# Where forty-eight groups of modulation rows are computed: the last eight move from the gaps about a layer norm into the pairs of the gated unit

## The reference, cut to what matters

```python
def adaln_params(cond, w, b):
    mod = (jax.nn.silu(cond) @ w + b)[:, None, :]
    return jnp.split(mod, 6, axis=-1)

def conformer_conv(h, w_in, b_in, dw_w, dw_b, ln_g, ln_b, w_out, b_out):
    a, gt = jnp.split(h @ w_in + b_in, 2, axis=-1)
    z = a * jax.nn.sigmoid(gt)
    z = depthwise_conv(z, dw_w, dw_b)          # 31 taps
    z = jax.nn.silu(layer_norm(z, ln_g, ln_b))
    return z @ w_out + b_out
...
    h = h + g1 * rms_norm(y, norm_g[i, 1])
    f = conv_ffn(rms_norm(h, norm_g[i, 2]) * (1.0 + sc2) + sh2, ...)
```

## Time and profile before

| | |
|---|---|
| median of three timed executions | 3034.64 us |
| profiled execution, its own time | 3032.49 us |
| its span in the profile | 3030.7 us |
| PE busy | 2747.4 us (91%) |
| DVE busy | 2064.8 us (68%) |
| ACT busy | 1280.9 us (42%) |
| mean granted TensorE clock | 0.954 of full speed |

### The profile page before, as it was taken

The page is one execution under the profiler, slowest core; times in us unless marked ns, Lnnn a source line. Parts: engine busy times, 40 slices in busy tenths (PEclk is TensorE's granted clock), DMA queues, the critical chain, the costliest instruction groups (busy, mean ns, idle before and its releaser), DMA issues. The chain is left out here.

```text
span 3030.7 us, 44962 instructions
## 1 busy us (share of the span) xinstructions
PE 2747.4 (91%) x17388; PEld 2473.3 (82%) x17388; DVE 2064.8 (68%) x2883; ACT 1280.9 (42%) x1888; POOL 132.4 (4%) x177
## 2 busy tenths in 40 slices
PE   5898888999999989999988498999899999999996
PEld 3888776999998989999976366777889999878785
DVE  3899988888975565655745547666478457584665
ACT  4231244433445353333431527777554334443332
POOL 0000000000000000000000002333000000000000
PEclk7999988999999999999998798999999999999998
DMA  6444422222221212222221120000122322233332
GB/s 261 152 160 146 149 102 89 79 84 92 90 77 65 81 56 89 79 87 94 71 89 56 42 76 9 1 1 1 56 84 85 97 97 88 94 95 120 97 97 83
DMA packets 66519, 263.14 MB, mean 87 GB/s; under 512 B 6960, under 2 KB 7216, under 8 KB 60080
## 3 DMA queue, kind: packets, MB, share of 16 engines
q1 hardware_dynamic: 58368, 213.17, 21.4%
q0 software_dynamic: 5760, 41.95, 3.9%
q10 hardware_dynamic: 2224, 5.69, 0.5%
HBM read 256.58 MB, written 4.19 MB: 86 GB/s over the span
## 5 line engine op out<-in xcount | busy, mean ns | idle before, releaser
L1603 PE MATMUL PS<-a_hi,w_hi 128*128 128x322 f32 (+7 forms) x3584 | 922.8, 326 | 113.5 <-DVE w_lo L962 58.4
L1603 PE MATMUL PS<-a_lo,w_hi 128*128 128x322 f32 (+7 forms) x3584 | 905.4, 321 | 0.0
L1603 PE MATMUL PS<-a_hi,w_lo 128*128 128x322 f32 (+7 forms) x3584 | 904.0, 321 | 0.0
L1603 PEld LDWEIGHTS PS<-a_hi,w_hi 128*128 128x128 f32 x3584 | 617.8, 194 | 168.7 <-DVE w_lo L962 73.2
L1603 PEld LDWEIGHTS PS<-a_lo,w_hi 128*128 128x128 f32 x3584 | 620.5, 194 | 25.2 <-issue 2.1
L1603 PEld LDWEIGHTS PS<-a_hi,w_lo 128*128 128x128 f32 x3584 | 617.1, 193 | 25.3
L962 DVE TENSOR_TENSOR w_lo<-raw,w_hi 128x1024 fp32r<-128x1024 f32 (+2 forms) x380 | 443.3, 1171 | 224.1 <-ACT w_hi L481 217.5
L481 ACT ACTIVATE w_hi<-raw 128x1024 fp32r<-128x1024 f32 (+2 forms) x380 | 385.7, 1015 | 1.6 <-DVE zB L1474 1.4
L1603 PE MATMUL PS<-z_hi,w_hi 128*128 128x320 f32 (+1 forms) x1056 | 301.3, 340 | 30.4 <-DVE z_lo L1351 28.3
L1603 PE MATMUL PS<-z_lo,w_hi 128*128 128x320 f32 (+1 forms) x1056 | 299.2, 338 | 0.0
L1603 PE MATMUL PS<-z_hi,w_lo 128*128 128x320 f32 (+1 forms) x1056 | 299.0, 338 | 0.0
(11 more groups left out here) (242 smaller groups left out, 3126.0 us busy)
## 6 DMA issues: line engine op xcount, KB each, us to landing
raw<-wstream SPq DMA_DIRECT2D x380, 512.0 KB, 3.5
ada_slot<-adastream POOLq DMA_DIRECT2D x40, 1024.0 KB, 5.2
ada_first<-adastream SPq DMA_DIRECT2D x4, 2048.0 KB, 19.8
h<-xT SPq DMA_DIRECT2D x1, 2640.0 KB, 14.6
h<-xT ACTq DMA_DIRECT2D x1, 2480.0 KB, 9.9
out<-h ACTq DMA_DIRECT2D x1, 2048.0 KB, 9.3
out<-h SPq DMA_DIRECT2D x4, 512.0 KB, 2.7
rope_sb<-rope ACTq DMA_DIRECT2D x1, 1024.0 KB, 4.9
```

Of the source, the lines that this page charges most:

```text
L1603: last = MM(PS[:, 2 * j + m, 0:n], wt[:, j, k, :], mv[:, k, m * n:(m + 1) * n], start=(k == 0 and p_ == 0), stop=(k == tiles - 1 and p_ == 2))
```

## The change

The four constants that said where the groups go become two tuples with the number of groups in each pair of the two gated stages. Stage A has 2, 2, 3, 3, 3, 3, 3, 2 (21 groups, 8 to 28), stage B has 3, 3, 3, 3, 2, 2, 2, 1 (19 groups, 29 to 47). A third group stands in the middle of a pair's first unit, ahead of k-tile 4; ACT copies it before it evacuates that unit. Nothing is left between stage B and cm but the turn of the last group, and nothing in the join.

```diff
-ADA_A, ADA_B, ADA_GAP, ADA_JOIN = 8, 24, 40, 42
+ADA_A, ADA_B = (2, 2, 3, 3, 3, 3, 3, 2), (3, 3, 3, 3, 2, 2, 2, 1)
...
                     for i in range(8):
-                        q, g, ga = q0 + i, x["g"] + i, x["ada"] + 2 * i
+                        q, g, rows = q0 + i, x["g"] + i, x["ada_n"][i]
+                        ga = x["ada"] + sum(x["ada_n"][:i])
+                        if rows == 3:
+                            ada_row_out(ga)
+                            ga += 1
...
                         split(q + 1, 1)
-                        ada_row_out(ga + 1)
+                        if rows > 1:
+                            ada_row_out(ga + 1)
...
                 if kind == "cm":
-                    for g in range(ADA_GAP, ADA_JOIN):
-                        ada_row_out(g)
                     cm_units(x)
                 if kind == "join":
-                    ada_row_out(ADA_JOIN)
                     root(s + 1, MIX, 2)
-                    for g in range(ADA_JOIN + 1, ADA_JOIN + 3):
-                        ada_row_out(g)
...
                     for m in range(4):
-                        if ADA_JOIN + 3 + m < N_MOD:
-                            ada_row_out(ADA_JOIN + 3 + m)
                         tiles = join_tiles(x, m)
...
-            def ada_group(g):
-
+            def ada_next(g):
+
+                if g > ADA_FIRST:
+                    ada_turn(g - 1)
                 ada_rows(g, ada_slot[g % 2])
-                ada_turn(g)
...
-                        unit(q, 0, a_hi, a_lo, w, KT, fresh=x["n"] - 1 if i == 0 else None)
+                        unit(q, 0, a_hi, a_lo, w, KT, {4: lambda g=ga: ada_next(g)} if rows == 3 else {},
+                             fresh=x["n"] - 1 if i == 0 else None)
...
-                        if ga > ADA_FIRST:
-                            ada_turn(ga - 1)
-                        ada_rows(ga, ada_slot[ga % 2])
+                        ga += rows == 3
+                        ada_next(ga)
                         unit(q, 1, a_hi, a_lo, w, KT)
-                        ada_turn(ga)
-                        ada_rows(ga + 1, ada_slot[(ga + 1) % 2])
+                        if rows > 1:
+                            ada_next(ga + 1)
                 if kind == "cm":
-                    ada_turn(ADA_GAP - 1)
-                    for g in range(ADA_GAP, ADA_JOIN):
-                        ada_group(g)
+                    ada_turn(N_MOD - 1)
...
                 if kind == "join":
-                    ada_rows(ADA_JOIN, ada_slot[ADA_JOIN % 2])
                     pe.wait_ge(evacuated, 2 * q0)
                     average_summed(7, rms[:, 0:MIX], MIX, 2)
-                    ada_turn(ADA_JOIN)
-                    for g in range(ADA_JOIN + 1, ADA_JOIN + 3):
-                        ada_group(g)
                     for k in range(KT):
                         pe.wait_ge(squared, x["sq"] + 8 + k + 1)
                         last = ones_product(t_mix[:, k], MIX, 2, k == 0, k == KT - 1)
                     last.then_inc(norm_step, 1)
-                    for g in range(ADA_JOIN + 3, N_MOD):
-                        ada_group(g)
```

More of the change, by code:

```diff
@@ L101, in plan @@
     ph = [dict(kind="pre", layer=0, which=0, chunk=glu_a, w=GA, t="T", first=True),
-          dict(kind="glu", chunk=glu_a, pairs=8, units=[("glu", 0, 8)], ada=ADA_A, host=pre_gb), pre_gb,
-          dict(kind="glu", chunk=glu_b, pairs=8, units=[("glu", 0, 8)], ada=ADA_B, host=ln_a), ln_a,
+          dict(kind="glu", chunk=glu_a, pairs=8, units=[("glu", 0, 8)], ada=ADA_FIRST, ada_n=ADA_A, host=pre_gb), pre_gb,
+          dict(kind="glu", chunk=glu_b, pairs=8, units=[("glu", 0, 8)], ada=ADA_FIRST + sum(ADA_A), ada_n=ADA_B, host=ln_a), ln_a,
           dict(kind="cm", chunk=mix_a, pairs=4, units=[("cm_out", 0, 4)], y="zA", sq=0, sums=0),
@@ L1266, in _ @@
                         if not pre and i == 1:
-                            modulation(0, 16, 48, ADA_B, 2)
+                            modulation(0, 16, 48, N_MOD // 2, 2)
                         conv((CONV_A if pre else CONV_B)[i])
@@ L1676, in _ @@
                     for i in range(8):
-                        q, ga = q0 + i, x["ada"] + 2 * i
+                        q, rows = q0 + i, x["ada_n"][i]
+                        ga = x["ada"] + sum(x["ada_n"][:i])
                         if host["kind"] == "pre" and i == 3:
```

## The result

The changed kernel took 3048.97 us (median of 12 executions, 3035.76 to 3051.13). The kernel before, timed beside it on the same chip, took 3034.58 (12 executions, 3032.4 to 3036.94). The ratio is 1.0037, with a 95% interval of 1.0025 to 1.0048. The forecast was 3036.5 with a range to 3042.0: the time is 12.5 us off and outside the range, and slower by more than 0.2%. The spread is a result of its own: these twelve executions of the kernel before stay within 4.5 us, the changed one covers 15 us, and its fastest execution is within the range of the kernel before.

The account below looks back on a forecast made before the run. PE and DVE were both nearly full in the gated stages, with PE idle behind them. Terms 6.0 + 1.2 - 3.6 - 1.9 + 0.2 gave +1.9 us: 3034.4 profiled, 3036.5 us median, range 3030.5 to 3042.

Parts of the forecast that it names:

- Price of a group: Each group inserted in a unit costs PE 1.5 us: turn and rows 1.43, one more entry some 0.1.
- Stage A: Five more groups in pairs three to seven, less what slack hides, cost +6.0 us, bounds 4.5 to 7.5.
- Stage B: Three more groups net, partly hidden by PE's slack, cost +1.2 us, between -0.75 and +3.8.
- the cold case: Stage B, pairs two and four: the same clock loss remains, costing +0.5 and +1.2, 1.7 us together.
- the warm case: Stage B, pair two: shorter idle time ahead, no clock loss, the 0.75 us DVE wait goes: -0.75 us.
- Gap ahead of cm: cm starts earlier; unit three's low weights limit the gain to 6.0, half-rate rows take 2.4: -3.6 us, between 3.1 and 4.2.
- Join: Without groups the first feed-forward unit ends 1.9 us earlier (1.4 to 2.3); the sums of squares lose 0.2.
- The feed-forward stage behind is PE-bound and keeps it.: Behind the join, PE sets the pace, so the feed-forward stage keeps the join's 1.9 us gain.
- the clock that falls more often: Rival: third groups break units in stages A and B; five more half-rate starts add 7.5 us, 3044 us; chance 0.13.
- hidden groups: Rival: third groups hide in PE's waits at pair ends, stage A costs 1 at most, 3031.5 us; chance 0.08.
- 13 us from the gap: Rival: the whole gap closes, cm starts 13 us earlier and keeps it, 3027 us; chance 0.08.
- late loads: Rival: group loads come 2 us late in each of nine pairs, some +15 us, 3051 us; chance 0.02.

Follow-up runs that it names:

- no8: Kernel before without the eight groups of the gap and join, two per pair kept, last 16 columns of layer 1's modulation set to 1: 3030.52 us, ratio 0.9986.
- a5: As `no8`, plus the five third groups of stage A, last six columns set to 1: 3040.07 us, ratio 1.001.
- the repeat: Changed kernel run again without edit: median 3047.04 us, ratio 1.0036; its second profiled execution took 3037.93 us.
- b3: As `no8`, but with stage B's groups as in the changed kernel, last ten columns set to 1: 3033.52 us, ratio 1.0.
- best: Kernel before with the eight groups moved: one more in stage B's pairs one, three, five, six, two behind each of cm's first two units: 3037.81 us, ratio 1.0014.
- b_pe18: Kernel before with eighteen extra PE products near 1200 us, 2.6 us of work, no group moved: 3041.61 us, ratio 1.0025.
- b_late2: Kernel before with two extra DVE reductions in the join, 1.5 us, no group moved: 3038.38 us, ratio 1.0011.
- b_pe6: Kernel before with six extra PE products near 1200 us, some 0.9 us of work, no group moved: 3037.7 us, ratio 1.0008.
- a_pe6: Changed kernel with six extra PE products near 1200 us, 0.9 us of work: 3046.44 us, ratio 1.0031.
- b_late1: Kernel before with one extra DVE reduction in the join, 0.8 us, no group moved: 3034.65 us, ratio 1.0001.
- b_again: Kernel before run again without edit, for a second profiled execution: 3034.36 us, ratio 0.9998.
- a_late3: Changed kernel with three extra DVE reductions in the join, 2.3 us: 3046.85 us, ratio 1.0042.

## Why the prediction was wrong, step by step

- **Price of a group, 1.5.** Right: 1.50 between the ends of pairs four and five. The prediction's remark on the page of the Trainium skill on column tiles ("TensorE: Matmul & The Clock Gate", Part 3) misreads the trace, though: the rows of a group do run side by side. Their 16 records stand in four sets of four; those of the first set start at 84.632, 84.639, 84.646 and 84.652 us, the next set at 84.872. What was wrong is the estimate of 0.4 us, which counted two sets where the trace has four. The sum went by the row and was not touched by it.
- **Stage A, +6.0.** Too small: 7.5 and 8.1, 7.7 above `no8` in `a5`. The slacks were read rightly (pairs three and four together, five, and seven are within 0.2 of the forecast in the profile after), but a new half-rate start came, worth 1.3 to 1.5, in pair six or seven. The bounds, 4.5 to 7.5, had room only for one such start fewer. That one, in pair eight, did go, and gave back 0.35 us where the bound had 1.5.
- **Stage B, +1.2 (-0.75 to +3.8).** Too small and inside its bounds: 1.9 to 3.6. Pairs two and four together cost 1.7 in the profile after, as the cold case said, and 0.5 in the repeat; the warm case of pair two came only in `b3`. Missed were 0.4 in pair one and 1.5 in pair eight, whose unit started at half rate; by `a5` and `best` this does not come from the missing group.
- **Gap ahead of cm, -3.6.** Right in mechanism, and in size within 0.6: -3.0 (just outside the stated 3.1 to 4.2) and -3.5; `no8` shows the 6.0 without the loss of clock as 5.8.
- **Join, -1.9 and +0.2.** -1.3 and -1.6 together; right within its bounds.
- **"The feed-forward stage behind is PE-bound and keeps it."** This is the step that failed. PE-bound it is, and PE's waits there kept their lengths. But a shift of a few microseconds moved these waits, and behind each of six the clock could fall differently: +9.3 us in the profiled execution after. I had looked at the clock only where the change puts instructions.
- **The rivals.** The nearest is the clock that falls more often, 3044 us. Its mechanism is the one that came, and its place was wrong: in stage A one half-rate start went and one came, in B pairs one, five and eight started with a lower clock than before, and most of the loss came in stages that the diff does not touch. It was priced at five falls and had a chance of 0.13; that its 3044 us lie nearer to the measured time than the forecast does is in part luck. The other three did not come: no hidden groups, no 13 us from the gap, no late loads.
- **The range** was built on terms up to 525 us, so its upper end, 3042, could not hold 3049.

In numbers: of the 15.0 us by which the profiled span missed the forecast sum (16.9 against 1.9), 1.0 was there ahead of any change, 4.9 came from the terms up to 525 us and 9.1 from behind.

The cause of the second part is shown as far as this: the loss arises without any moved group, from a delay alone (`b_pe18` by its times and its profile, `b_late2` by its profile), at waits whose length does not change, and it goes with the place of the waits against the clock's changes. What stays open is the exact rule by which a wait of 3.12 us costs 0, 1.5 or 2.8 us: of the forecasts made with theory P, those for `b_pe6`, `a_pe6` and `b_late1` and the places of the falls in `b_again` missed. Open, too, is why executions of one kernel take different courses, and how often: of the 18 executions of the changed kernel, eight lie between 3035.8 and 3044.4 us and ten between 3048.7 and 3051.1, and one of each kind was profiled. What is behind 2400 us, where five kernels (`no8`, `b3`, `b_late1`, `b_late2`, `a_late3`) get 2.2 to 2.9 us back, was not looked into.

## What to carry to other kernels

When a change shifts a later stage, list PE's waits of about 1.5 to 10 us in all that follows and count for each a half-rate start gained or lost (0.7 to 2.8 us here), in both directions, even if nothing there is edited; that widens the range beyond the bounds of the local terms. A small gain is best judged by several profiled executions and by the spread of the times: of the kernels with work removed or better placed, `no8` kept 4 of its 5.9 us in the median and `best` none of its 2.6.

## What the runs showed of the hardware that was not expected

- One and the same wait of PE (3.12 us for `z_lo`) was followed by a granted clock of 1.00, 0.86 or 0.75 over the next 12 us, in kernels whose products there are the same. The Trainium skill, "TensorE: Matmul & The Clock Gate", in "Why this matters for your kernels", says that idle gaps between bursts of products should be kept short so that the clock stays up. The runs agree in kind; they add that a gap of one length can cost nothing or 2.8 us.
- Half-rate starts came after idle times as short as 0.57 us (pair eight of stage B, with another idle time of 2.2 us shortly ahead) and 1.68 us (stage A), and failed to come after 3.12 us. The wait's place against the clock's changes sorts the cases: with the same 7.18 us of waiting at 957 us, five profiles in which the fall came 3.94 to 4.01 us ahead of the next product lost nothing there, and eight with 4.21 to 4.89 us lost 1.1 to 1.4 us behind it.
- More work could be free: 2.3 us added to the changed kernel (`a_late3`) left its median where it was, 3046.85 against 3048.97 and 3047.04.
- The kernel before is steadier against such effects than the changed one, but not free of them: of its 107 executions in all rounds, 98 lie between 3032.1 and 3038 us and nine between 3038 and 3044.7; the changed kernel spreads over 15 us in 18. Up to the join `b_late1` and `b_late2` are the kernel before, and at 403 us they stood at +2.0 and +3.8, 2.2 and 1.6 of it from stage A. Why most executions of the kernel before come back to one place against the clock's changes is not explained here.
